# A transformer kernel: the first MLP pair with tokens stationary, behind an output product ordered by token block

## What is computed

```python
def first_block(...):
    ...
        y = mixer(h, w_in[l], conv_a[l], ...)          # ends with @ w_out
        x = x + rmsnorm(y, norm_mix_post[l])
        h = rmsnorm(x, norm_ffn_pre[l])
        y = conv_mlp(h, w_up[l], conv_ffn[l], w_down[l])
        x = x + rmsnorm(y, norm_ffn_post[l])
```

## Time and profile before

| | |
|---|---|
| median of 3 runs | 684.61 us (683.48 to 685.54) |
| profiled execution: its time | 682.7 us |
| profiled execution: span | 680.7 us |
| PE / DVE / ACT busy | 637.0 / 379.1 / 277.7 us |
| granted TensorE clock, mean | 0.985 |

### The profile page before, as it was taken

How to read it: one execution, slowest core, us unless ns; L and a number is a source line. 1 busy time by engine, 2 the same in 40 slices (tenths; PEclk the granted TensorE clock), 3 DMA queues, 4 the chain that set the end, 5 groups by cost and what they waited for, 6 DMA issues and landing times.

```text
span 680.7 us, 11095 instructions
## 1 busy us (share of the span) xinstructions
PE 637.0 (94%) x4347; PEld 482.7 (71%) x4347; DVE 379.1 (56%) x666; ACT 277.7 (41%) x431; POOL 56.1 (8%) x81
## 2 busy tenths in 40 slices
PE   7999999999999999999999999999999987668895
PEld 4999997799999999996598788744444432315364
DVE  5696965768766666666769456352222221203195
ACT  6763373656555555545774831220111110000193
POOL 1000000400000000002074620000000000000010
PEclk9999999999999999999999999999999998898998
DMA  9943542747655555302933448899899999999931
GB/s 323 328 172 126 194 141 67 267 149 243 235 186 185 185 185 186 128 0 101 392 142 123 139 172 320 350 430 428 354 430 430 425 425 428 428 428 427 405 128 62
DMA packets 55208, 174.75 MB, mean 257 GB/s; under 512 B 4742, under 2 KB 29442, under 8 KB 48898
## 3 DMA queue, kind: packets, MB, share of 16 engines
q1 hardware_dynamic: 54496, 172.54, 66.2%
q10 hardware_dynamic: 674, 1.69, 0.7%
HBM read 173.17 MB, written 1.05 MB: 256 GB/s over the span
## 4 chain that ended last, share of the span: by engine, by line
PE 73%; DMA 14%; DVE 7%; ACT 2%; issue 2%; another core or an unknown queue 0%; POOL 0%; POOLq 0%; DVEq 0%; ACTq 0%
PE ps L1809 15%; PE ps L1811 15%; PE ps L1810 15%; DMA W<-in_w_moe_dram 7%; DMA spare<-in_w_moe_dram 6%; PE ps L2326 6%; PE ps L2310 3%; PE ps L2386 3%; PE ps L2332 2%; PE ps L2006 2%; PE ps L1781 1%; PE ps L2433 1%; PE ps L2154 1%; DVE arena L1466 1%; PE ps L2105 1%
## 5 line engine op out<-in xcount | busy, mean ns | idle before, releaser
L1809 PE MATMUL ps<-hT_high,w_up_parts 128*128 128x256 f32 x352 | 99.9, 284 | 0.0
L1811 PE MATMUL ps<-hT_high,w_up_parts 128*128 128x256 f32 x352 | 99.7, 283 | 0.0
L1810 PE MATMUL ps<-hT_low,w_up_parts 128*128 128x256 f32 x352 | 99.7, 283 | 0.0
L1809 PEld LDWEIGHTS ps<-hT_high,w_up_parts 128*128 128x128 f32 x352 | 67.6, 192 | 0.5
L1810 PEld LDWEIGHTS ps<-hT_low,w_up_parts 128*128 128x128 f32 x352 | 67.6, 192 | 0.4
L1811 PEld LDWEIGHTS ps<-hT_high,w_up_parts 128*128 128x128 f32 x352 | 67.6, 192 | 0.0
L1297 DVE TENSOR_TENSOR w_up_parts<-W,w_up_parts 128x1024 fp32r<-128x1024 f32 x44 | 53.2, 1235 | 24.3 <-ACT w_up_parts L826 24.3
L826 ACT CAST w_up_parts<-W 128x1024 fp32r<-128x1024 f32 x44 | 44.7, 1047 | 28.5 <-PE ps L1811 28.5
L2326 PE MATMUL ps<-W,junk 128*32 128x512 f32 x368 | 46.2, 630 | 7.5 <-DMA W<-in_w_moe_dram 7.5
L996 ACT ACTIVATE sg<-ps 128x256 f32<-128x256 f32 x9 | 3.5, 384 | 121.4 <-PE ps L2326 121.4
L1809 PE MATMUL ps<-h_high,dense_high 128*128 128x256 f32 x160 | 45.8, 286 | 0.0
(11 more groups left out here) (480 smaller groups left out, 1318.7 us busy)
## 6 DMA issues: line engine op xcount, KB each, us to landing
W<-in_w_moe_dram SPq DMA_DIRECT2D x22, 2048.0 KB, 21.1
arena<-in_w_moe_dram SPq DMA_DIRECT2D x14, 2048.0 KB, 30.0
W<-in_w_up_dram SPq DMA_DIRECT2D x22, 1024.0 KB, 8.8
W<-in_w_in_dram SPq DMA_DIRECT2D x8, 2048.0 KB, 10.9
W<-in_w_down_dram SPq DMA_DIRECT2D x11, 1024.0 KB, 5.1
spare<-in_w_moe_dram SPq DMA_DIRECT2D x5, 2048.0 KB, 20.7
hh<-in_w_moe_dram SPq DMA_DIRECT2D x4, 2048.0 KB, 32.7
W<-in_w_out_dram SPq DMA_DIRECT2D x2, 2048.0 KB, 9.3
```

The costliest lines, as they stand in the source:

```text
L1809: pe.matmul(o, lhs[0], rhs[0], start=first, stop=False, skip_group_check=True)
L1810: pe.matmul(o, lhs[0], rhs[1], start=False, stop=False, skip_group_check=True)
L1811: return pe.matmul(o, lhs[1], rhs[0], start=False, stop=last_k, skip_group_check=True)
```

## The change

The output product ends block 0 after 60 matmuls instead of 72: block 1's second half is done late, its last 12 matmuls behind the turn of block 0. All four tiles of pair 0 are split ahead of the hand-over (y's high part is put elsewhere, since it lay where tiles 2 and 3 go). Block 0's turned activations are scaled, rounded and lowered directly behind its own hand-over. For pair 0 alone PE then has the tokens stationary and the weights moving: block 0 with all four tiles in one matmul of 512 columns (24 of them), block 1 in two lots of two tiles (48 of 256 columns). The result has tokens on partitions, so ACT copies it out of PSUM (`copy_up`, three copies) and PE turns it back (16 transposes of 128 x 128) into banks 0 and 1, where the convolution reads it. Block 1's eight transposes stand behind tile 0 of pair 1. The filler matmuls between the two turns go. The first turn of PE's loop over pairs is written out.

```diff
@@ -76,7 +76,7 @@
                 ("scores_done", 4), ("kot_done", 2), ("gv_done", 2), ("kv_done", 3), ("gb_done", 2),
-                ("o_done", 2), ("go_done", 2), ("onT_done", 2)),
+                ("o_done", 2), ("go_done", 2), ("onT_done", 2), ("u_done", 3), ("u_turned", 1)),
     "pe_mix2": (("c_done", 2), ("xm_done", 2), ("cT_done", 2), ("turned_done", 1), ("z2_done", 2),
@@ -84,7 +84,7 @@
                  ("exp_ready", 4), ("gc_ready", 2), ("kot_ready", 2), ("gb_ready", 2),
-                 ("osq_ready", 1), ("ostd_ready", 1), ("sgo_ready", 2)),
+                 ("osq_ready", 1), ("ostd_ready", 1), ("sgo_ready", 2), ("uc_ready", 3)),
     "act_mix2": (("cs_ready", 1), ("cstd_ready", 1), ("gln_ready", 1), ("xm_ready", 2), ("sz_ready", 2),
@@ -213,7 +213,7 @@
 h1 = [v3(rounded("h1_high", junk_at, 0, 2 * D), KD), v3(rounded("h1_low", hh_at, 0, 2 * D), KD)]
-y1 = [v3(rounded("y1_high", arena_at, Q_IN, 2 * D), KD), v3(rounded("y1_low", hh_at, 2 * D, 2 * D), KD)]
+y1 = [v3(rounded("y1_high", arena_at, NAR - UNIT, 2 * D), KD), v3(rounded("y1_low", hh_at, 2 * D, 2 * D), KD)]
@@ -725,8 +725,6 @@
            .then_inc(sig("ystd_ready"), 1)
-        if b == 1 and r == 0:
-            round_h(0)
         c = 4 * (r + 1) + b
@@ -825,12 +823,28 @@
-    split_up(0, 0, 0, (0, 1))
+    split_up(0, 0, 0)
     for b in range(TB):
         hand_over(0, b)
-    act.dma_start(gbc[:], a["norm_ffn_post"][0:1, :].broadcast_to([P, D])).then_inc(sig("gbc_landed"), 16)
-    for j in range(1, 4):
-        round_h(j)
+        if b == 1:
+            act.dma_start(gbc[:], a["norm_ffn_post"][0:1, :].broadcast_to([P, D])).then_inc(sig("gbc_landed"), 16)
+        else:
+            round_h(0)
+            round_h(1)
+    def copy_up(n, b, c0, c1):
+        act.wait_ge(sig("u_done"), at("u_done", n))
+        act.copy(junk[:, 512 * b + c0 * P:512 * b + c1 * P], ps[:, 5 if b and not c0 else 4, c0 * P:c1 * P]).then_inc(sig("uc_ready"), 1)
+    copy_up(1, 0, 0, 4)
+    round_h(2)
+    round_h(3)
+    copy_up(2, 1, 0, 2)
+    split_up(1, 1, 0, (0, 1))
+    copy_up(3, 1, 2, 4)
+    split_up(1, 1, 0, (2, 3))
+    act.wait_ge(sig("u_turned"), at("u_turned", 1))
@@ -856,9 +870,7 @@
-    act.wait_ge(sig("x_ready"), 2)
-    split_up(0, 0, 0, (2, 3))
-    conv_mlp(0, 0, 0)
+    conv_mlp(0, 0, 0, False)
     with act.Fori(0, NPAIR // 2 - 1) as i:
@@ -1134,7 +1146,7 @@
                                      ALU.add).then_inc(sig("yms_ready"), 1)
-            if b == 1:
+            if b == 1 and r == 1:
                 turn_out(r + 1, gain, 0)
@@ -1150,15 +1162,19 @@
                                      ALU.add).then_inc(sig("xms_ready"), 1)
-            if b == 1 and r == 0:
-                lower_h(0)
             dve.wait_ge(sig("std_ready"), 2 * (r + 1) + b + 1)
...
                               ALU.mult).then_inc(sig("hn_ready"), 1)
-        turn_out(r + 1, gain, 2)
-        turn_out(r + 1, gain, 3)
+            if r == 0:
+                for j in (2 * b, 2 * b + 1):
+                    turn_out(r + 1, gain, j)
+                for j in (2 * b, 2 * b + 1):
+                    lower_h(j)
+        if r == 1:
+            turn_out(r + 1, gain, 2)
+            turn_out(r + 1, gain, 3)
@@ -1297,10 +1313,8 @@
-    split_up(0, 0, (0, 1))
+    split_up(0, 0)
     hand_over(0, "norm_ffn_pre")
-    for j in range(1, 4):
-        lower_h(j)
@@ -1336,7 +1350,6 @@
     dve.sem_inc(sig("uact_ready"), 1)
-    split_up(0, 0, (2, 3))
     conv_mlp(0, 0, 0)
@@ -1928,42 +1941,75 @@
     pe.wait_ge(sig("sgo_ready"), at("sgo_ready", 2))
-    for half in range(2):
-        for b in range(TB):
-            for k in range(4):
-                pe.wait_ge(sig("dense_low"), 4 * (6 + half) + k // 2 + 1)
-                product(ps[:, 4 + 2 * b + half, :], [t[:, k, b * P:(b + 1) * P] for t in y1],
-                        [t[:, k, :] for t in panel_hl(6 + half)], k == 0, False)
-    for b in range(TB):
-        pe.wait_ge(sig("y1_low"), b + 2)
-        for half in range(2):
-            for k in range(4, KD):
-                pe.wait_ge(sig("dense_low"), 4 * (6 + half) + k // 2 + 1)
-                last = product(ps[:, 4 + 2 * b + half, :], [t[:, k, b * P:(b + 1) * P] for t in y1],
-                               [t[:, k, :] for t in panel_hl(6 + half)], False, k == KD - 1)
-        last.then_inc(sig("y_done"), 1)
+    def out_rows(b, half, ks):
+        for k in ks:
+            pe.wait_ge(sig("dense_low"), 4 * (6 + half) + k // 2 + 1)
+            last = product(ps[:, 4 + 2 * b + half, :], [t[:, k, b * P:(b + 1) * P] for t in y1],
+                           [t[:, k, :] for t in panel_hl(6 + half)], k == 0, k == KD - 1)
+        return last
+    out_rows(0, 0, range(4))
+    out_rows(1, 0, range(4))
+    out_rows(0, 1, range(4))
+    pe.wait_ge(sig("y1_low"), 2)
+    out_rows(0, 0, range(4, KD))
+    out_rows(0, 1, range(4, KD)).then_inc(sig("y_done"), 1)
+    out_rows(1, 1, range(4))
+    pe.wait_ge(sig("y1_low"), 3)
+    out_rows(1, 0, range(4, KD))
     turn_h(1, 0)
-    keep_busy(3, 8)
-    for k in range(24):
-        pe.matmul(ps[:, 3, 0:P], y1[0][:, k % KD, 0:P], y1[0][:, k % KD, 0:P], start=True, stop=True, skip_group_check=True)
+    out_rows(1, 1, range(4, KD)).then_inc(sig("y_done"), 1)
+    u_tok = v3(junk[:], TB)
+    def up_tokens(b, c0, c1):
+        pe.wait_ge(sig("up_low"), c1)
+        for k in range(KD):
+            if k % 4 == 0:
+                pe.wait_ge(sig("hT_low"), 2 * b + k // 4 + 1)
+            last = product(ps[:, 5 if b and not c0 else 4, c0 * P:c1 * P], [t[:, k, b * P:(b + 1) * P] for t in hT_hl],
+                           [t[:, c0:c1, k, :] for t in w_up_hl], k == 0, k == KD - 1)
+        return last
+    def turn_up(b, c0, c1):
+        for c in range(c0, c1):
+            i, g = divmod(c, 2)
+            last = pe.transpose(ps[:, i, 256 * g + b * P:256 * g + (b + 1) * P], u_tok[:, b, c * P:(c + 1) * P], ident[:])
+        return last
+    up_tokens(0, 0, 4).then_inc(sig("u_done"), 1)
     turn_h(1, 1)
-    pe.wait_ge(sig("hT_ready"), 4 + 2)
-    keep_busy(0, 8)
     pe.wait_ge(sig("x_ready"), 2)
-    for n in range(4):
-        pe.matmul(ps[:, 4 + n, :], zb[:, 0:P], zb[:], start=True, stop=False, skip_group_check=True)
-    def up(p, q):
-        if not (isinstance(p, int) and p == 0):
-            pe.wait_ge(sig("tap_done"), p * 8 - 7)
+    for n in range(2):
+        pe.matmul(ps[:, 6 + n, :], zb[:, 0:P], zb[:], start=True, stop=False, skip_group_check=True)
+    pe.wait_ge(sig("uc_ready"), at("uc_ready", 1))
+    turn_up(0, 0, 4)
+    for h in range(2):
+        last = up_tokens(1, 2 * h, 2 * h + 2)
+        last.then_inc(sig("u_done"), 1)
+        pe.sem_inc(sig("up_used"), 2)
+    def last_turns():
+        pe.wait_ge(sig("uc_ready"), at("uc_ready", 2))
+        turn_up(1, 0, 2)
+        pe.wait_ge(sig("uc_ready"), at("uc_ready", 3))
+        turn_up(1, 2, 4).then_inc(sig("u_turned"), 1)
+        for n in range(2):
+            pe.matmul(ps[:, 4 + n, :], zb[:, 0:P], zb[:], start=True, stop=False, skip_group_check=True)
+    def up(p, q, behind_first=None):
+        pe.wait_ge(sig("tap_done"), p * 8 - 7)
         for c in range(4):
+            if c == 1 and behind_first:
+                behind_first()
             pe.wait_ge(sig("up_low"), p * 4 + c + 1)
...
             for k in range(KD):
-                if isinstance(p, int) and p == 0 and c == 0 and k % 4 == 0:
-                    pe.wait_ge(sig("hT_low"), 3 + k // 4)
                 last = product(o, [t[:, c, k, :] for t in w_up_hl], [t[:, k, :] for t in hT_hl], k == 0, k == KD - 1)
@@ -1978,8 +2024,11 @@
     pe.sem_inc(sig("down_used"), 1)
-    up(0, 0)
-    with pe.Fori(0, NPAIR // 2) as i:
+    up(1, 1, last_turns)
+    down(0, 0)
+    up(2, 0)
+    down(1, 1)
+    with pe.Fori(1, NPAIR // 2) as i:
         up(i * 2 + 1, 1)
```

## The result

The changed kernel has a median of 677.72 us over 4 runs (676.83 to 678.65), the kernel before 684.74 over 4; the ratio is 0.9895, with a 95% interval of 0.9877 to 0.9913. The medians lie 7.0 us apart, where 4.7 was forecast. The profiled execution took 678.28 with a span of 676.4, so the two profiles differ by 4.3 to 4.4 only. Over all that was run for this study, the change took 678.39 on average in 20 executions (standard deviation 1.5), the kernel before 684.87 in 78 (0.7): **6.5 less, plus or minus 0.7**. One execution of the kernel before, of 2590 us, is far off all others and left out of every figure here.

What follows compares the result with a forecast made beforehand. PE was taken as the bound, 73% of the last-ending chain and never idle in an MLP stretch. Terms of -0.5, -5.7 and +1.5 us gave -4.7: 678.0 profiled, median 679.9, range 677.7 to 682.3.

Steps and rivals of the forecast that it cites:

- the sum: From the output product to the first down product: -0.5, -5.7 and +1.5, together -4.7 us.
- the step from the sum to the median: Whole kernel: profiled execution 682.7, 1.9 below the median of 684.61; with -4.7 it takes 678.0, the median 679.9.
- Output product: Its 96 matmuls keep a pace of 0.233; block 0 ends 2.8 us sooner, block 1's hand-over begins 1.1 later.
- Block 1's hand-over: It takes 5.6 us instead of 6.7, winning back the 1.1 of its later start: net 0.
- half a microsecond: Margin by which block 0's moved steps end before block 1's hand-over; a rival without it, 681 to 682, chance 0.1.
- Under the hand-over: Block 0's 24 matmuls of 512 columns take 5.6 us at 0.233, fitting into PE's fillers and idle time.
- the rival at 0.50: Products with tokens stationary: the operand in pieces goes at f32's pace, +7.9 us, 692.5, chance 0.05.
- Pair 0's second half: Block 1's 48 matmuls of 256 columns take 6.2 us instead of 11.9: -5.7.
- Behind the turn, and the copies: After block 1's turn, pair 0's second half starts 0.5 us earlier; from its end to the scaled copies, 1.5 more.
- the first rival: Up to the first down product: the gain is that of PE alone, 5.5 to 5.9 us, giving 679.0, chance 0.1.
- Kept afterwards: Behind the first down product: pair 2's weights make ACT start 1.4 us late, within 2.8 of room, cost 0.
- The clock: Rival around the turns: without fillers PE's clock falls, costing 1.7 us, so -3.0 and 681.6, chance 0.06.

Runs made afterwards that it cites:

- The old order: The changed kernel with the output product's matmuls in their old order and block 0's turn after all of them: ratio 0.9946 to the kernel before, mean 681.2 us.

## Why the prediction was right or wrong

The direction and the mechanism were right, the size was too small: 677.72 was at the very edge of the range (677.7), and by the ratio the change came out at 684.61 x 0.9895 = 677.4, below it. Two steps of the prediction were too small. One is the sum: it had -4.7 up to the first down product, where the profiles show -5.2. The other is the step from the sum to the median ("with -4.7 it would take 678.0, and the median 679.9"), which took the gain in the stage for the whole gain: 0.2 came in the MLP behind it, and 1.1 more in the mean of all executions, which no profile shows. The second weighs more: with -5.2 in the sum the same reckoning gives 679.4. Chance had a part in it too, since the first four executions average 677.7 and all twenty 678.4, which lies in the range.

The sum term by term: start of pair 0's second half -0.7 (predicted -0.5), the second half itself -5.9 (-5.7), between its end and the scaled copies +1.4 (+1.5), from there to the down product -0.1 (0). The steps, all counted from the output product's first matmul (96.65 in the prediction, 96.57 measured):

| | predicted | measured |
|---|---|---|
| block 0's hand-over begins (DVE) | 14.3 | 14.0 |
| block 1's hand-over begins | 23.7 | 23.3 |
| its hn complete | 29.3 | 29.0 |
| pair 0's second half begins | 32.0 | 31.7 |
| ACT sees its end | 38.2 | 37.7 |
| scaled copies | 42.2 | 41.7 |
| first down product | 51.7 | 51.1 |

- **Output product: mis-sized, the one cause found for the stage's part.** "95 steps [...] are a pace of 0.233", and all its new times were made of that. In the change 59 steps take 110.07 - 96.57 = 13.5, 0.229 each. The text costed the splitting of the tiles that the move of y made possible, and the move itself not at all. The kernel with y alone moved shows that it is worth 0.4 to 0.5 us there. In the change about 0.3 of it is there in the first two lines of the table, half of the missing 0.6 of the last line: PE's first turn, 116.02 - 96.57 = 19.45 behind the start, came only 0.1 ahead of the prediction's 19.6.
- **Block 1's hand-over: right.** 5.62 was taken over from block 0, and it took 125.53 - 119.91 = 5.62. The moved steps ended at 118.09 + 1.29 = 119.38, half a microsecond ahead, as worked out. The old order showed what that half microsecond is worth.
- **Under the hand-over: right.** The operand in four pieces of 128 columns goes at (125.38 - 119.71) / 24 = 0.236 including the change to the turn, little over the contiguous one's 0.229 without any; the rival at 0.50 fell. The pieces lie 2048 words apart and not 1024 (in w_up_parts a tile's high and low part, 1024 words each, stand behind each other).
- **Pair 0's second half: 0.1 to 0.2 too long in the sum.** It took 134.31 - 128.29 = 6.0, where 6.2 was forecast and 11.9 was measured before.
- **Behind the turn, and the copies: right** to a tenth or two. ACT's copy of 512 columns took 0.57, the two of 256 0.37 each (0.39 expected); PE waited 0.91 for uact_low (about 1 expected). The early split of w_down showed that this chain and not PE was the limit, worth 1.1. One count was wrong without harm: ahead of the down product the text has "8 transposes (1.0)" on PE, and there are four. So PE alone would have given more than the 5.5 to 5.9 of the first rival; the stage of 50.0 is 6.3 under before.
- **Kept afterwards: right.** ACT waited 1.87 for pair 2's weights and began at 148.68, where 148.7 had been worked out; up to the last down product nothing of the gain was lost.
- **The clock: the rival fell.** It stayed full without the fillers, from 119.6 to 147.6 with 16 transposes and two waits of 0.9 in it, one of them at its end. The Trainium skill's statement that transposes don't count as busy time ("TensorE: Matmul & The Clock Gate", part 4) isn't refuted by this, since matmuls lay on both sides; it was no reason to fear for this change.
- **The addition to the median.** 4.7 was taken from a profile whose execution, 682.7, was faster than any of the kernel's 78 others (682.9 to 686.1). For one stage that did no harm, since 56.3 came again; for the whole it supposed that what other executions lose beside the profiled one, the change loses too. The means above say 1.9 for before and 0.6 for the change; why is open.

## What to carry to other kernels

When one engine waits for a chain of small steps that begins with a half of its data, compute the part of the next product that needs the first half only, even if the operands must change roles: the copies out and the turns back put 1.4 us on the path here, a copy and a second cast, against the 5.9 that they made room for. Moving a buffer is an edit of its own and can change the pace of the matmuls that read it; look at the distance of their starts before and after. And when moved steps have to fit in ahead of a signal, work out the margin, since beyond it the delay is paid in full (2.1 us in the old order).

## What was not expected of the hardware

The same 96 matmuls of 128 x 128 by 512 went at 0.233 with y's high part, one of the stationary operands, at one address (two profiles), at the same 0.233 with it 1024 words further (one) and at 0.228 at the end of the arena (two profiles in which the 96 run through). Full matmuls of the same kind elsewhere in the program, such as the down products, mostly had 0.227. I don't know the cause.
